# Two-layer decoder trunk in fp32r: down projections of the middle feed-forward groups on TensorE's two row halves

## What is computed

```python
D_MODEL = 2048; SEQ = 256; D_FF = 5632

def swiglu_ffn(h, w_gate_up, w_down):
    gu = h @ w_gate_up
    gate, up = gu[..., :D_FF], gu[..., D_FF:]
    return (jax.nn.silu(gate) * up) @ w_down

    h = rmsnorm(x, g[2])
    y = swiglu_ffn(h, ffn_w_gate_up[i], ffn_w_down[i])
    x = x + rmsnorm(y, g[3])
```

## Time and profile before

| | us |
|---|---|
| median of 3 runs | 2105.38 (2104.92 to 2105.56) |
| span of the profiled execution | 2104.5 |
| PE busy | 2094.2, 9603 matmul records |
| weight loads (PEld) busy | 1718.9 |
| DVE busy | 1615.4 |
| ACT busy | 1152.9 |
| POOL busy | 156.6 |
| moved by DMA | 425.01 MB, mean 202 GB/s |

### The profile page before, as it was taken

One profiled execution on the slowest core, in us unless ns is written; L12 is line 12 of the kernel. 1 busy time (PEld: TensorE's weight loads), 2 busy tenths in 40 slices (PEclk: granted clock), 3 DMA queues, 4 the chain that ended last, 5 costly groups with the idle time before them and its releaser, 6 DMA issues.

```text
span 2104.5 us, 32177 instructions
## 1 busy us (share of the span) xinstructions
PE 2094.2 (100%) x9603; PEld 1718.9 (82%) x9603; DVE 1615.4 (77%) x3299; ACT 1152.9 (55%) x2061; POOL 156.6 (7%) x311
## 2 busy tenths in 40 slices
PE   9999999999999999999999999999999999999998
PEld 7877888888888888888888887888888888888886
DVE  6798677887667776678898898577877668776686
ACT  7666565544455454555666555665544545445553
POOL 2110000000000000000152343000000000000000
PEclk9999999999999999999999999999999999999999
DMA  7699866665666655665687787756555665556662
GB/s 257 211 247 253 223 206 206 195 191 173 199 199 199 197 171 190 199 204 161 202 247 219 214 251 215 234 190 216 189 187 178 199 217 184 188 178 203 206 193 87
DMA packets 221564, 425.01 MB, mean 202 GB/s; under 512 B 15808, under 2 KB 25440, under 8 KB 220976
## 3 DMA queue, kind: packets, MB, share of 16 engines
q1 hardware_dynamic: 214528, 402.45, 61.6%
q0 software_dynamic: 6672, 21.31, 3.7%
q10 hardware_dynamic: 288, 0.33, 0.1%
HBM read 409.31 MB, written 14.71 MB: 201 GB/s over the span
## 4 chain that ended last, share of the span: by engine, by line
PE 97%; DMA 1%; issue 1%; SPq 1%; ACT 0%; POOL 0%; DVE 0%; POOLq 0%
PE bank L1338 31%; PE bank L1340 31%; PE bank L1339 31%; PE bank L1385 1%; PE bank L1410 1%; PE bank L1351 1%; DMA x_sb<-x 0%; DMA p_f<-first_scratch 0%; DMA stage<-swa_w_out 0%; PE bank L1368 0%; SPq L541 0%; SPq L566 0%; PE bank L1432 0%; PE bank L1429 0%; PE bank L1571 0%
## 5 line engine op out<-in xcount | busy, mean ns | idle before, releaser
L1338 PE MATMUL bank<-ring_hi,a_hi 128*128 128x512 f32 x2240 | 880.3, 393 | 0.5 <-DVE ring_lo L817 0.5
L1340 PE MATMUL bank<-ring_hi,a_lo 128*128 128x512 f32 x2240 | 873.1, 390 | 0.0
L1339 PE MATMUL bank<-ring_lo,a_hi 128*128 128x512 f32 x2240 | 872.8, 390 | 0.0
L607 ACT ACTIVATE ring_hi<-stage,g_t 128x512 fp32r<-128x512 f32 x992 | 661.2, 717 | 376.6 <-DMA stage<-ffn_w_gate_up 203.0
L817 DVE SCALAR_TENSOR_TENSOR ring_lo<-stage,g_t,ring_hi 128x512 fp32r<-128x512 f32 x992 | 708.5, 759 | 147.3 <-ACT ring_hi L607 144.9
L1338 PEld LDWEIGHTS bank<-ring_hi,a_hi 128*128 128x128 f32 x2240 | 420.9, 188 | 92.9 <-issue 5.9
L1340 PEld LDWEIGHTS bank<-ring_hi,a_lo 128*128 128x128 f32 x2240 | 420.8, 188 | 88.1
L1339 PEld LDWEIGHTS bank<-ring_lo,a_hi 128*128 128x128 f32 x2240 | 421.1, 188 | 84.7
L815 DVE TENSOR_TENSOR ring_lo<-stage,ring_hi 128x512 fp32r<-128x512 f32 x480 | 305.5, 687 | 139.9 <-ACT ring_hi L605 138.5
L605 ACT ACTIVATE ring_hi<-stage 128x512 fp32r<-128x512 f32 x480 | 278.4, 624 | 225.0 <-PE bank L1340 149.5
L1338 PE MATMUL bank<-ring_hi,h_hi 128*128 128x512 f32 x704 | 274.6, 390 | 0.0
(11 more groups left out here) (148 smaller groups left out, 836.6 us busy)
## 6 DMA issues: line engine op xcount, KB each, us to landing
stage<-ffn_w_gate_up SPq DMA_DIRECT2D x352, 512.0 KB, 4.6
stage<-ffn_w_down SPq DMA_DIRECT2D x176, 512.0 KB, 5.5
stage<-fox_w_in SPq DMA_DIRECT2D x96, 512.0 KB, 4.7
stage<-swa_w_in SPq DMA_DIRECT2D x48, 512.0 KB, 4.7
stage<-swa_w_out SPq DMA_DIRECT2D x64, 256.0 KB, 6.2
stage<-fox_w_out SPq DMA_DIRECT2D x32, 512.0 KB, 5.5
first_scratch<-first_blocks SPq DMA_DIRECT2D x16, 384.0 KB, 5.4
p_f<-first_scratch SPq DMA_DIRECT2D x64, 96.0 KB, 3.9
```

What stands on the lines that cost most here:

```text
L607: nc.scalar.activation(ring_hi[:, n % RING, :], src, ACT.Identity, scale=g_t[:, row * KT + j:row * KT + j + 1]).then_inc(hi_ready, 1)
L1338: nc.tensor.matmul(dst, hi_a, hi_w, start=start, stop=False)
L1339: nc.tensor.matmul(dst, hi_a, lo_w, start=False, stop=False)
L1340: return nc.tensor.matmul(dst, lo_a, hi_w, start=False, stop=stop)
```

## The change

In the down units of the middle groups (g = 1 to 9 of both layers) each of the three matmuls of a product becomes two of 64 rows: rows 0 to 63 into bank n, rows 64 to 127 into bank 4 + n. Lower and upper half alternate. VectorE then adds first bank n and after it bank 4 + n to `y_sb`; the second add waits for the first by a new semaphore, `y_upper`, and only the second one counts up `y_added`. All other units, and the first and the last group, are as before.

```diff
+        y_upper = sem("y_upper")
...
+        def by_row_halves(u):
+
+            ffn = ffn_part(u)
+            return ffn is not None and ffn[2] == 2 and 0 < ffn[1] < FG - 1
...
                 if g == 0:
                     nc.vector.tensor_copy(dst, main[n][:, :]).then_inc(y_added, 1)
+                elif by_row_halves(u):
+                    dve.wait_ge(y_added, 8 * (f - 1) + k + 1 + 8 * i)
+                    nc.vector.tensor_tensor(dst, main[n][:, :], dst, ALU.add).then_inc(y_upper, 1)
+                    dve.wait_ge(y_upper, 8 * (f - f // FG * 2 - 1) + k + 1 + 8 * i)
+                    nc.vector.tensor_tensor(dst, bank[4 + n][:, :], dst, ALU.add).then_inc(y_added, 1)
                 else:
...
+            def product_by_row_halves(dsts, hi_a, lo_a, hi_w, lo_w, start, stop):
+
+                for left, right, first, end in ((hi_a, hi_w, start, False), (hi_a, lo_w, False, False), (lo_a, hi_w, False, stop)):
+                    for rows, dst in zip((slice(0, P // 2), slice(P // 2, P)), dsts):
+                        last = nc.tensor.matmul(dst, left[rows], right[rows], start=first, stop=end)
+                return last
...
-                    last = product(dst[:, :], a_h[:, k, tok(t)], a_l[:, k, tok(t)], ring_hi[:, n % RING, :], ring_lo[:, n % RING, :],
-                                   k == 0, k == n_k - 1)
+                    operands = (a_h[:, k, tok(t)], a_l[:, k, tok(t)], ring_hi[:, n % RING, :], ring_lo[:, n % RING, :], k == 0, k == n_k - 1)
+                    if by_row_halves(u):
+                        last = product_by_row_halves((dst[:, :], bank[4 + j // 4][:, :]), *operands)
+                    else:
+                        last = product(dst[:, :], *operands)
```

## The result

The changed kernel takes 2114.37 us (median of 3, 2113.61 to 2114.61) against 2105.38: 9.0 us more, a ratio of 1.004 with a 95% interval of 1.0027 to 1.0054. The direction and the mechanism are those of the prediction (2113), and the size is near it; one term was too small.

The account below looks back on a forecast made before the run. The prediction took TensorE's own pace as the only bound. Changeovers at +7.3 us, with pairs, issue and adds at 0 each, on 2105.4 gave 2112.7, stated as 2113 us; the range was 2094 to 2138.

Parts of the forecast that it names:

- The bound: In the changed stretch only TensorE's own pace counts, unless the change makes a new wait.
- The halves run together: In the changed down units two 64-row halves run at the same time, as the attention score pairs do.
- The rival without overlap: Halves in the down units do not overlap in fp32r: +392 us, 2504; chance 0.09.
- The pair's price, 0 us: In the changed down units a pair of halves takes 0.2267 us, like one full matmul: 0 us.
- Both bounds, 0.217 and 0.240: Microseconds a pair in the down units: with the score pairs' extra (-16.8 us), or both halves' extras counted (+23.2 us).
- the rivals built on them (2096, 2136): Pair in the down units faster, 0.217 us: -9.5 us, chance 0.27; or slower, 0.240 us: +30.5 us, chance 0.13.
- The changeover, 18 x 0.41 = 7.3 us: Each of 18 down units goes from 128 to 64 rows and back once, 0.41 us together: +7.3 us.
- The adds, 0 us: VectorE's 144 new adds in the down units, 0.72 us each, delay nothing TensorE waits for: 0 us.
- The thinnest cover: In a down unit, h_lo of the second token tile keeps 0.83 us of slack behind one new add.
- Issue: A down unit has 192 matmuls to issue, one per 113 ns, a rate the sequencer has been seen at: 0 us.

Follow-up runs that it names:

- the kernel with whole groups: Changed kernel with gate and up units of the middle groups in row halves too, their upper sums left out of the result: 2106.29 us, ratio 1.0001.
- the kernel with late h_lo: Changed kernel with three further dependent VectorE instructions ahead of h_lo of the second token tile in the 18 units: 2136.9 us.

## Why the prediction was right, and where it was off

*The bound.* Right: TensorE's pace and nothing else; every microsecond of the result is in its stream, without a new wait.

*The halves run together.* Right, and taken from the score pairs of another format and half the column rate. The rival without overlap (2504) was not reached even with the order of the halves changed.

*The pair's price, 0 us.* Right, and to the digit: 576 halves in 65.28 us as 288 full ones. The reason given (each half has its own chain of load, swap and stream) agrees with the lower half that runs alone at the same pace; the chains themselves no trace shows. Both bounds, 0.217 and 0.240, and the rivals built on them (2096, 2136) fell with it.

*The changeover, 18 x 0.41 = 7.3 us.* The mechanism was right, and this is the term that was mis-sized: it measured 0.49 us, 8.8 in all. The 0.41 came from the second full matmul behind a score block. By then 0.20 us a side are spent, but the pace is not back: in the changed kernel the next steps are 0.23 to 0.24 us (901.97, 902.20, 902.44 and 923.97, 924.21), and at the eleventh matmul 0.25 us are lost, some 0.045 us a side more. The trace of before would have given only a part of it. Taken to the eleventh full matmul behind the block, the block of 16 adds 1053.99 - 1049.77 - 11 x 0.2267 = 1.73 us and that of 8 adds 1288.72 - 1285.14 - 2.49 = 1.09, which makes 1.09 - (1.73 - 1.09) = 0.45 for in and out. The score pairs are plain float32, so slow steps of fp32r pairs behind the way in cannot show there. With 0.49 the sum would have been 2114.2. Also, the prediction takes its second value of 0.41 for a confirmation, and it is none: the 0.65 us of the pairs is the difference of the two blocks, so the block of 16 gives the same 0.41 by construction.

*The adds, 0 us.* Right: the kernel with the adds alone has the time of before. The step of 0.72 us measured 0.73; VectorE's busy time in a group rose by 54.36 - 48.87 = 5.5 us, and its idle time fell by 5.0 where 5.8 was said, the group being 0.49 us longer. The thinnest cover was h_lo, as said, but 1.06 us and not 0.83, because TensorE's own changeover comes first.

*Issue.* No cost at 113 ns an instruction, for 590 us on end in the kernel with whole groups.

## To carry to other kernels

Splitting a full 128-row product into two row halves that run side by side is neutral in time here: it gives nothing and costs nothing as long as TensorE stays in that shape and VectorE has room for the adds. What costs is the change of shape, 0.25 us each way, so count the changes, not the matmuls, and keep work of one shape together. Price such a disturbance to the point where the pace is back, not to the next instruction; and check by leaving one part of the change away at a time, since adds, pairs and changeovers came in one edit and only one of them was paid for.

## What was not expected of the hardware

TensorE pairs a half with one that stands three places later in its program at no cost (2113.82 us), and where twelve and twelve stand it starts an upper half ahead of three lower ones, not more. The two halves need not alternate strictly, but must be near.

After a change of rows the fp32r pace needs about ten matmuls at up to 0.24 us to come back to 0.2267: of the 0.25 us that a change costs, 0.20 are lost by the second matmul and the rest by the eleventh. Behind the wait in the kernel with late h_lo the next steps are long in the same way (0.33, then 0.23 to 0.24).
